# A hybrid decoder layer on eight cores: one tile at a time against list-scheduled groups of four tiles with transposes by DMA and streamed weights

## The reference

```python
def layer_norm(x, g, b):
    xf = x.astype(jnp.float32)
    mu = jnp.mean(xf, axis=-1, keepdims=True)
    var = jnp.mean(jnp.square(xf - mu), axis=-1, keepdims=True)
    y = (xf - mu) * lax.rsqrt(var + EPS) * g.astype(jnp.float32) + b.astype(jnp.float32)
...
def hgrn2_chunk(state, inp):
...
    b = jnp.cumsum(log_f, axis=2)                    # inclusive log decay within chunk, <= 0
...
    o_inter = jnp.einsum('bhck,bhkv->bhcv', q * jnp.exp(b), state)
...
    a_diag = jnp.einsum('bhntk,bhnsk,bhntsk->bhnts', qs, ks, decay)
    o_diag = jnp.einsum('bhnts,bhnsv->bhntv', a_diag, vs)
...
    a_off = jnp.einsum('bhntk,bhnsk->bhnts', q_off, k_off)
    o_off = jnp.einsum('bhnts,bhsv->bhntv', a_off, v)
    o = o_inter + (o_diag + o_off).reshape(B, H, C, V)
    new_state = state * jnp.exp(b_last)[..., None] + jnp.einsum(
        'bhck,bhcv->bhkv', k * jnp.exp(b_last[:, :, None] - b), v)
    return new_state, o
...
def hgrn2_mixer(q_raw, f_raw, i_raw, g_raw, lower_bound, norm_g, valid):
...
    q = jax.nn.silu(q_raw.astype(f32))
    fg = lower_bound + (1.0 - lower_bound) * jax.nn.sigmoid(f_raw.astype(f32))
    m = valid[None, :, None]
    log_f = jnp.where(m, jnp.log(fg), 0.0)           # pad slots: identity transition
...
    k = jnp.where(m, 1.0 - fg, 0.0)                  # input gate tied to forget gate; pads write nothing
...
    o = o * lax.rsqrt(jnp.mean(o * o, axis=-1, keepdims=True) + EPS) * norm_g.astype(f32)
    gate = jax.nn.silu(g_raw.astype(f32)).reshape(B, P, HG_HEADS, HG_V)
    return (o * gate).reshape(B, P, HG_VW).astype(q_raw.dtype)
...
def swa_sink_attention(q_raw, k_raw, v_raw, sinks, pos):
...
    q = rope(q_raw.reshape(B, P, ATT_HEADS, HEAD_DIM), pos).astype(f32)
    k = rope(k_raw.reshape(B, P, ATT_KV_HEADS, HEAD_DIM), pos).astype(f32)
    v = v_raw.reshape(B, P, ATT_KV_HEADS, HEAD_DIM).astype(f32)
    scale = HEAD_DIM ** -0.5
...
    band_ok = (key_pos >= N_META) & (key_pos <= qp) & (qp - key_pos < WINDOW)
    meta_ok = meta_pos <= qp                       # meta tokens always visible (causally)
...
    p = jax.nn.softmax(jnp.concatenate([s_meta, s_band, sink], axis=-1), axis=-1)
...
    o = (jnp.einsum('bnhgqm,bmhd->bnqhgd', p_meta, v_meta)
         + jnp.einsum('bnhgqk,bnkhd->bnqhgd', p_band, v_band))
    return o.reshape(B, P, ATT_QW).astype(q_raw.dtype)
...
        proj = h @ w_in[l]                                   # single combined input projection
        hq, hf, hi, hg, aq, ak, av, gates = jnp.split(proj, split_idx, axis=-1)
        y_hg = hgrn2_mixer(hq, hf, hi, hg, lbs[l], hg_norm_g[l], valid) @ w_branch_hg[l]
        y_att = swa_sink_attention(aq, ak, av, attn_sinks[l], pos) @ w_branch_attn[l]
        g_hg, g_att = jnp.split(jax.nn.sigmoid(gates), N_BRANCH, axis=-1)
        mix = (g_hg * y_hg + g_att * y_att) @ w_out[l]
        h = layer_norm(ALPHA * h + mix, ln1_g[l], ln1_b[l])
        a, u = jnp.split(h @ w_ffn_in[l], 2, axis=-1)
        h = layer_norm(ALPHA * h + (jax.nn.silu(a) * u) @ w_ffn_out[l], ln2_g[l], ln2_b[l])
    return h[:, BLOCK:]
```

## Time and profile before

| | |
|---|---|
| runs | 4988.68, 4994.0 and 4994.34 us, median 4994.0 |
| the profiled execution | 5015.8 us (slowest of eight cores; 4970.0 to 5015.8) |
| PE busy | 4311.7 us, 86% |
| DVE busy | 2566.4 us, 51% |
| ACT busy | 1584.3 us, 32% |
| POOL busy | 557.2 us, 11% |
| DMA | 243.09 MB, 48 GB/s on the mean |

### The profile page before, as it was taken

How to read it: one execution, slowest core, us unless ns; L and a number is a source line. 1 busy time by engine, 2 the same in 40 slices (tenths; PEclk the granted TensorE clock), 3 DMA queues, 4 the chain that set the end, 5 groups by cost and what they waited for, 6 DMA issues and landing times.

```text
span 5015.8 us, 65133 instructions; the slowest of 8 cores (4970.0 to 5015.8 us)
## 1 busy us (share of the span) xinstructions
PE 4311.7 (86%) x22787; PEld 2046.9 (41%) x22787; DVE 2566.4 (51%) x4615; ACT 1584.3 (32%) x2827; POOL 557.2 (11%) x677
## 2 busy tenths in 40 slices
PE   0798888888888888888888873999999999999998
PEld 0344444444444444444444431444444444444443
DVE  2355666666665666666665641444444444444444
ACT  2344444444444444444444430111111111111111
POOL 0011111111111111111111110000000000000000
PEclk9678999999999999999999986999999999999999
DMA  8006321000001000000000005111111111111110
GB/s 254 15 34 90 71 53 49 34 34 33 27 31 34 34 34 34 34 34 34 28 29 34 34 20 178 42 43 42 43 43 42 43 43 43 46 47 51 44 49 34
DMA packets 86113, 243.09 MB, mean 48 GB/s; under 512 B 10160, under 2 KB 19632, under 8 KB 84928
## 3 DMA queue, kind: packets, MB, share of 16 engines
q1 hardware_dynamic: 84448, 221.62, 13.1%
q0 software_dynamic: 1344, 17.30, 2.6%
HBM read 172.30 MB, written 101.19 MB: 55 GB/s over the span
## 4 chain that ended last, share of the span: by engine, by line
PE 69%; DVE 9%; ACT 8%; issue 8%; DMA 4%; POOL 1%; DVEq 0%; SPq 0%; ACTq 0%; POOLq 0%
PE ps L425 19%; PE ps L995 13%; PE ps L966 11%; PE ps L969 11%; PE ps L803 5%; PE ps L776 2%; PE ps L409 2%; ACT L503 2%; PE ps L506 1%; ACT hbf L476 1%; ACT mT L413 1%; ACT hT L413 1%; PE ps L509 1%; ACT thG L764 1%; PE ps L516 1%
## 5 line engine op out<-in xcount | busy, mean ns | idle before, releaser
L425 PE MATMUL ps<-win,hT 128*128 128x512 bf16 (+1 forms) x5160 | 1329.3, 409 | 55.9 <-ACT hT L413 55.9
L425 PEld LDWEIGHTS ps<-win,hT 128*128 128x128 bf16 x5160 | 516.7, 106 | 635.0 <-issue 280.9
L966 PE MATMUL ps<-hTg,wfi 128*128 128x512 bf16 x2816 | 666.9, 380 | 98.9 <-issue 78.3
L974 ACT ACTIVATE tha<-ps 128x512 bf16<-128x512 f32 x352 | 210.5, 598 | 1655.6 <-PE ps L969 1607.5
L995 PE MATMUL ps<-wfo,gT 128*128 128x512 bf16 x2816 | 631.1, 388 | 42.7 <-DVE gT L981 38.8
L969 PE MATMUL ps<-hTg,wfi 128*128 128x512 bf16 x2816 | 665.6, 379 | 0.0
L977 DVE SCALAR_TENSOR_TENSOR s2b<-tha,ps 128x512 f32<-128x512 bf16 x352 | 241.9, 687 | 669.3 <-ACT tha L974 669.2
L966 PEld LDWEIGHTS ps<-hTg,wfi 128*128 128x128 bf16 x2816 | 274.6, 98 | 435.8 <-issue 108.2
L995 PEld LDWEIGHTS ps<-wfo,gT 128*128 128x128 bf16 x2816 | 279.4, 100 | 394.4 <-issue 78.1
L969 PEld LDWEIGHTS ps<-hTg,wfi 128*128 128x128 bf16 x2816 | 275.7, 98 | 332.9 <-issue 1.1
L803 PE MATMUL ps<-wo,mT 128*128 128x512 bf16 x1024 | 240.9, 390 | 59.3 <-ACT mT L413 59.3
(11 more groups left out here) (174 smaller groups left out, 5539.6 us busy)
## 6 DMA issues: line engine op xcount, KB each, us to landing
h_scr<-r SPq DMA_DIRECT2D x64, 512.0 KB, 2.6
h1in<-h_scr SPq DMA_DIRECT2D x64, 512.0 KB, 4.1
x_1<-x SPq DMA_DIRECT2D x32, 512.0 KB, 3.7
x_0<-x SPq DMA_DIRECT2D x32, 512.0 KB, 3.8
h1T_scr<-h1T SPq DMA_DIRECT2D x64, 256.0 KB, 2.2
hTg<-h1T_scr SPq DMA_DIRECT2D x64, 256.0 KB, 2.7
y_out<-rr_0 SPq DMA_DIRECT2D x32, 512.0 KB, 2.9
y_out<-rr_1 SPq DMA_DIRECT2D x32, 512.0 KB, 2.9
```

Of the source, the lines that this page charges most:

```text
L425: inst = e.matmul(psb(bk)[:, 0:ncols], hTt[:, c, :], win_sb[:, c, col0:col0 + ncols], start=(c == 0), stop=(c == 7))
L966: inst = e.matmul(psb(ba)[:, 0:ntok], wfi_sb[:, c, j * 128:(j + 1) * 128], hTg[gi][:, 0:ntl, c, :], start=(c == 0), stop=(c == 7))
L974: S2.op("act", lambda e: e.activation(out=tha[ai][:, 0:ntok], in_=psb(ba)[:, 0:ntok], func=AF.Tanh, scale=0.5), reads=[Bbank2[ba]], writes ...
```

## The change

The kernel is written anew; reference, inputs and the split over cores stay.

**Order.** Every operation carries a cost in ns and its place in the program. `schedule` is a list scheduler: it keeps a clock per engine and takes, among the operations that are ready by then, the earliest in the program for which a PSUM bank is free (pools: pairs of banks for projections, a pair for the attention, single banks for the recurrence). Costs are constants in the code. The program's order from which it starts treats groups of four tiles, 16 of them: recurrence (`stage2`) and attention (`stage3`) of group g are merged with the first projections of group g+1 (`s12`), then come the gates and branches of g (`stage4`) with the first norm of g+2 (`stage0`), then the output projection (`stage5`). The meta tokens are handled apart, 16 rows alone.

**Layout.** Query and forget projections (`hgrn_qf`), gates and branches are computed channel-major, 128 channels by the 512 tokens of a group, so that the outputs `mT` and the inputs of the recurrence need no transposes. The cumulative decay is a `tensor_tensor_scan` on VectorE. The chunk of the recurrence is 128 tokens in one step. The attention's products with the values have 64 outputs by 512 columns; a matrix of ones gives the denominators in the same form, the sink is a row of `Em`, and the division is a reciprocal of 128 x 512 and a multiplication.

**Transposes.** What stays token-major is transposed by DMA, four a tile in pass 1 (`hT`, `qkT`, `ktok`, `ogT`) and one in pass 2 (`h1T`), all issued by SP.

**Weights.** DMAs on GpSimd's queue cast all weights to bf16 in HBM or SBUF. `wv`, `whg`, `waq`, `wakv` and `wo` stay in SBUF in pass 1, `wfo` in pass 2. Query, forget, gate, branch and FFN-in weights are read from HBM again for each group, through a ring of 11 slots (`ring`).

**Boundary.** The fence between the passes is gone. Pass 1 stores the residual sum, and the norm after it is now in pass 2 (`stage6`). ScalarE computes Silu in one step there, and VectorE one operation per block instead of two. The output product of the FFN is cut in two halves over j.

```diff
-            def transposes(src_fn, n, dst2, BdstT, Bsrc, evac_eng, bk):
...
-                def pe_fn(e):
-                    inst = None
-                    for i in range(n):
-                        inst = e.transpose(pv[:, i * 128:(i + 1) * 128], src_fn(i), ident[:])
-                    return inst
...
-                if evac_eng == "act":
-                    S.op("act", lambda e: e.copy(out=dst2, in_=pv[:, 0:n * 128]), reads=[Bbank[bk]], writes=[BdstT])
...
-                S.op("pe", lambda e: e.matmul(psb(bP), T64, lnf[:], start=True, stop=True),
-                     reads=[Blnf, B_const], writes=[Bbank[bP]])
...
-                S.cur = lB1 = []
-                if t < NT:
-                    do_B1(t)
-                S.cur = lA = []
-                if t + 1 < NT:
-                    do_A(t + 1)
-                extra = []
-                if t >= min(6, NT):
-                    take = len(cv_ops) if t == NT else 3
-                    extra, cv_ops[:] = cv_ops[:take], cv_ops[take:]
-                order += merge3([lB2, lB1, lA, extra]) if PIPELINE else (lB2 + lB1 + lA + extra)
...
+    def schedule(self, pools):
...
+                for s, i, o in heapq.nsmallest(12, cand[e]):
+                    t, _ = bank_at(o)
+                    if t is None:
+                        continue
+                    t = max(t, free[e])
+                    if o.tab is not None and cur not in o.tab:
+                        t = max(t, o.ready + self.PATIENCE)
+                    if pick is None or t < pick[0]:
+                        pick = (t, o)
+                    if t <= free[e]:
+                        break
...
+    def cast_dma(dst, src, writes, nbytes):
...
+        dma(lambda e: e.dma_start(out=dst, in_=src), [], list(writes) + [cvB[k]], "cv%d" % k, nbytes, cost=1100,
+            eng="pool")
...
+    def ring_load(nslots, src, Bsrc):
+        at = rg["at"]
+        if at + nslots > RING:
+            at = 0
+        rg["at"] = at + nslots
+        bs = Bring[at:at + nslots]
+        dma(lambda e: e.dma_start(out=ring[:, at:at + nslots, :].rearrange("p a b -> p (a b)"), in_=src), Bsrc, bs,
+            "rg%d" % at, nslots * 2048 * 128)
+        flat = ring[:, at:at + nslots, :].rearrange("p a b -> p (a b)")
...
+    def stage0T(t, g, s):
+        kb = t % 4
+        dst = hT[g % 2]
+        dma(lambda e: e.dma_start_transpose(out=dst[:, :, s * 128:(s + 1) * 128], in_=hbf[kb][:]), [Bhbf[kb]],
+            [BhT[g % 2][s]], "hT%d_%d" % (g % 2, s), 262144, cost=1200)
...
+        dma(lambda e: e.dma_start_transpose(out=qkT[kt][:], in_=qkr[kr][:]), [Bqkr[kr]], [BqkT[kt]], "qkT%d" % kt,
+            163840, cost=1200)
...
+    def hgrn_qf(h, g, w, Bw, ntok):
...
+        S.op("dve", lambda e: e.tensor_tensor_scan(out=lb_[:, 0:ntok], data0=rm[:, 0:ntok], data1=lb_[:, 0:ntok],
+                                                   initial=0.0, op0=ALU.mult, op1=ALU.add),
+             [Blb, Brm], [Blb], cost=2 * dve(512))
...
+    def stage2(t, g, s):
...
+        dma(lambda e: e.dma_start_transpose(out=ktok[i2][:], in_=kd[:, s, :, :].rearrange("p h t -> p (h t)")), Bkd,
+            [Bktok[i2]], "kt%d" % i2, 131072, cost=1200)
...
+        def fR(e):
+            inst = None
+            for h in range(4):
+                inst = e.tensor_scalar(out=R32[:, h, :], in0=Tst[:, h, :], scalar1=dap[:, h:h + 1],
+                                       scalar2=cie[:, h:h + 1], op0=ALU.mult, op1=ALU.mult)
...
+        dma(lambda e: e.dma_start_transpose(out=ogT[:, :, s * 128:(s + 1) * 128], in_=og[i2][:]), [Bog[i2]],
+            [BogT[s]], "ogT%d" % s, 131072, cost=1200)
...
+    def stage3(t, g, s):
...
+        def fpv(e):
+            inst = None
+            for i, (E, _, v, _, on, _) in enumerate(kinds):
+                for q in range(2):
+                    inst = e.matmul(bank(P)[q * 64:(q + 1) * 64, :], v[:, q * 64:(q + 1) * 64], E[:, q, :],
+                                    start=(i == 0), stop=(i == n - 1))
+                for q in range(2):
+                    inst = e.matmul(bank(P, 1)[q * 64:(q + 1) * 64, :], on[:], E[:, q, :], start=(i == 0),
+                                    stop=(i == n - 1))
+            return inst
...
+        S.op("dve", lambda e: e.reciprocal(out=rd[:], in_=bank(P, 1)), [P.sub[1]], [Brd], cost=3380)
+        S.op("dve", lambda e: e.tensor_tensor(out=aoT[:, :, s * 128:(s + 1) * 128],
+                                              in0=bank(P).rearrange("p (j q) -> p j q", j=4),
+                                              in1=rd[:].rearrange("p (j q) -> p j q", j=4), op=ALU.mult),
+             [P.sub[0], Brd], [BaoT[s]], cost=dve(512))
...
+    def stage4(c, g, nt):
+        w, Bw = ring_load(3, wgb_d[c], Bwgb[c])
...
+        def fg_(k):
+            def f(e):
+                inst = None
+                for kc in range(8):
+                    inst = e.matmul(bank(P, k)[:, 0:ntok], w[:, kc * 256 + k * 128:kc * 256 + (k + 1) * 128],
+                                    hTg[:, kc, 0:ntok], start=(kc == 0), stop=(kc == 7))
+                return inst
+            return f
...
+        def fy(e):
+            inst = None
+            for h in range(4):
+                inst = e.matmul(bank(Y)[:, 0:ntok], w[:, 2048 + h * 128:2048 + (h + 1) * 128], ogT[:, h, 0:ntok],
+                                start=(h == 0), stop=(h == 3))
+            for h in range(4):
+                inst = e.matmul(bank(Y, 1)[:, 0:ntok], w[:, 2560 + h * 128:2560 + (h + 1) * 128], aoT[:, h, 0:ntok],
+                                start=(h == 0), stop=(h == 3))
+            return inst
...
+        S.op("dve", lambda e: e.scalar_tensor_tensor(out=m12[:], in0=thG[i2][:], scalar=1.0, in1=pair(Y),
+                                                     op0=ALU.add, op1=ALU.mult), [BthG[i2]] + Y.sub, [Bm12],
+             cost=dve(1024))
+        S.op("pool", lambda e: e.tensor_tensor(out=mT[:, c, :], in0=m12[:, 0:512], in1=m12[:, 512:1024],
+                                               op=ALU.add), [Bm12], [BmT[c]], cost=1210)
...
+    def stage5(t, g, s):
...
+        S.op("dve", lambda e: e.scalar_tensor_tensor(out=xb[:], in0=pair(P), scalar=0.5 / ALPHA, in1=xb[:],
+                                                     op0=ALU.mult, op1=ALU.add), P.sub + [Bxb], [Bxb],
+             cost=dve(1024))
+        dma(lambda e: e.dma_start(out=r_d[t * 128:(t + 1) * 128, :], in_=xb[:]), [Bxb], [Br_d[t]], "rs%d" % k, 524288)
...
+    for g in range(NG):
+        la = recs([(stage2, t, g, s) for s, t in enumerate(groups[g])])
+        lb = recs([(stage3, t, g, s) for s, t in enumerate(groups[g])])
+        lc = s12(g + 1) if g + 1 < NG else []
+        ops += merge(la, lb, lc)
+        l4 = recs([(stage4, c, g, len(groups[g])) for c in range(8)])
+        l0 = recs([(stage0, t, g + 2, s) for s, t in enumerate(groups[g + 2])]) if g + 2 < NG else []
+        ncv = len(ffn_cv) if g == NG - 1 else (4 if g >= 1 else 0)
+        cv, ffn_cv[:] = ffn_cv[:ncv], ffn_cv[ncv:]
+        ops += merge(l4, l0, cv)
+        l5 = recs([(stage5, t, g, s) for s, t in enumerate(groups[g])])
+        l0 = recs([(stage0T, t, g + 2, s) for s, t in enumerate(groups[g + 2])]) if g + 2 < NG else []
+        ops += merge(l5, l0)
...
+    def stage6(t, g, s):
...
+        dma(lambda e: e.dma_start_transpose(out=h1T[g % 2][:, :, s * 128:(s + 1) * 128], in_=h1b[kb][:]), [Bh1b[kb]],
+            [Bh1T[g % 2][s]], "h1T%d_%d" % (g % 2, s), 262144, cost=1200)
...
+    def ffn_in(j, g, nt, gslots):
+        w, Bw = ring_load(2, wfi_d[j], [Bwfi_d[j]])
...
+        S.op("act", lambda e: e.activation(out=sl[i][:, 0:ntok], in_=bank(P)[:, 0:ntok], func=AF.Silu), [P.sub[0]],
+             [Bsl[i]], cost=act(512), tab="S")
...
+            for a in range(0, NJ, 11):
+                js = list(range(a, min(a + 11, NJ)))
+                S.op("pe", fo(n, js), [BgT[gslots[j]] for j in js] + [Bwfo[j] for j in js], [P.sub[n]],
+                     cost=MM(len(js)))
...
+    S.schedule({"P": [0, 2], "S": [4], "H": [6, 7], "F": [0, 2, 4, 6]})
```

1813 lines of the change are left out of this document (963 added, 850 removed).

## The result

The changed kernel takes 4247.45 us as a median of four runs against 4994.17 (4233.4 without the run at 4699.98); the ratio is 0.849, 95% interval 0.846 to 0.853.

The account below looks back on a forecast made before the run. TensorE was taken to bound both passes, with VectorE nearly equal outside pass 1's gates. Start 75, groups 2000, turn 15, pass 2 1864 and tail 12 sum to 3966 us, as a median 3950; range 3780 to 4090, with (a) to 4400.

Parts of the forecast that it names:

- The groups: Pass 1: 125 us a group, from 33 for gates and branches plus 78 at 85% busy TensorE (92); 16 groups 2000.
- VectorE: Pass 1: VectorE's work sums to 21.2 us a tile (18.5 to 23), 85 a group, below TensorE's 111.
- The start: Before the steady groups: weights load while TensorE has work for about half; 75 us over the steady pace (50 to 120).
- The turn: Between the passes: only the normalisation of four tiles stands in the way; 15 us (5 to 30) instead of 78.
- Pass 2 and tail: Pass 2 at 116.5 us a group (114.5 to 121), 1864 in all; tail after the last product 12 us.
- The signs: Listed measurements that would show the forecast right, such as groups of 120 to 130 us and TensorE near 88%.
- (a): Rival: VectorE and the chain bind pass 1; a group takes 130 to 150 us, total 4190; chance 0.30.
- (b): Rival: DMA transposes bind SP's queue; at 12 us each total 5270; chance 0.05 up to the old time, 0.07 beyond.
- (c): Rival: denser work lowers the clock on all cores, groups at 145 and 140 us, total 4640; chance 0.04.
- (d): Rival: weights stream slower, in pass 2 at 100 GB/s instead of 145, 168 us a group, total 4770; chance 0.03.

Follow-up runs that it names:

- e1: The changed kernel with each cast of the FFN weights made to wait for its group's first merge: 4202.6 us, ratio 0.841.
- e5: As e1, but the scheduler is told that the FFN casts move no bytes: 4226.1 us, ratio 0.847.
- e9: As e5, with two casts under way at a time instead of four: 4182.1 us, ratio 0.838.
- e12: As e11, with one cast under way at a time instead of two: ratio 0.837.
- e13: The changed kernel with FFN casts held for their group's first merge (priced), one cast at a time, and xB at the end of pass 1's memory: 4090.7 us, 0.818.
- e11: As e10, with the residual buffers xB laid at the end of pass 1's memory, no longer under h1: ratio 0.838.
- e10: As e9, with a group's four FFN casts waiting for its last merge instead of its first: 4218.1 us, ratio 0.845.

## Why the prediction was right or wrong

**The groups: right in mechanism, 5.8 us too low each.** The split was: gates 33, the rest 78 of TensorE's work at 85% busy. Measured: 37.3 and 93.5, with TensorE at 83% of the rest (the gates' stretch runs at full clock and is longer because it holds 177 products and not the 152 that I counted, so the sum of both is the better measure). TensorE's busy time is 115.0, forecast 111. The attention's products were 0.9 us a tile cheaper than I took (a pair at 0.22, below the lower bound of 0.31 that I read from the scores); so 107.4 would have been due, 7.6 less than measured. Most of the 7.6 is the clock, 0.94 outside the gates, which I had priced only as a rival. The attention's query projection shows it in one group, first behind a wait, then at once behind other products:

```profile
1240.40 0.59 PE L89 MATMUL ps<-waq,hT_88 128*128 128x512 bf16 x1 [5.64 <-ACT og_121 L933]
1240.78 3.19 PE L704 MATMUL ps<-waq,hT_88 128*128 128x512 bf16 x7
...
1274.36 1.67 PE L704 MATMUL ps<-waq,hT_88 128*128 128x512 bf16 x7
```

The same seven products take 3.19 us at the lower of the two levels (1.2 GHz) and 1.67 at the upper; added up over seven groups, what products took beyond their time at full clock is some 5 to 6 us a group, an estimate from the rows. The idle time, 15.8 us a group, is 1.8 over the 14 in the forecast (92 - 78). So the 5.8 us too many are -3.6 for the attention, +7.6 and +1.8; for the whole of pass 1 that is 93 us.

**VectorE: right in the sum, partly by luck.** It is busy 85.2 us a group, forecast 85. But the forecast added up durations of single operations (its terms as listed give 20.9 a tile, not 21.2), and measured so a tile takes 22.7 (635.7 us for 28 tiles); the busy time is less because operations overlap. The reciprocal (2.6 taken, 3.35 measured, inside 0.69 to 4.4) and the four products with two scalars (0.22 taken, 0.44 on the mean) were under; the scan (1.4 taken, 1.19 and 1.66) was right on the mean.

**The start: the step that failed.** I took 11 and 14 MB at the pace of one row, let TensorE work half of that time, and wrote that the streams fit, with landings that grow. Three things were wrong in it. The FFN's 17 MB stood nowhere in this term, because I read their place in the program and not in the order in which GpSimd issues them: some 86 us (e1). Transfers were priced by bytes, while with four casts in flight loads of x and the slowest transposes land late, and the first tiles go through x, a norm, a transpose and a product one after another: the first branch product comes 20 us earlier with half as many, 64 with a quarter, 27 of which the next group loses again (e5, e9, e12). And TensorE did not work half: 55.6 of the first 200 us. What remains of the 263 after these steps is not settled; in e13 start and casts together are still 203 us (2252.9 less 16 groups of 128.1).

**The turn: mis-sized.** 15 taken (5 to 30), 36.8 measured. The norms that I named were not the wait; the loads ahead of them stood behind `xB`, over which `h1` lies in memory (e11). That lies in the code, and no row of before could show it.

**Pass 2 and tail: right, a little over.** 114.2 us a group against 116.5, just under the range of 114.5 to 121; TensorE was busy for 500 of 500 us, so the gaps that I had left in (116.5 - 113.9) were not there.

**The signs.** TensorE at 88% (804.74 of 915.63), VectorE's 21 us a tile and the reciprocal came as I wrote. Groups of 120 to 130 us, a clock of 0.96 or more, pass 2 at 115 to 118 a group and less than 30 us between the passes did not.

**The rivals.** (a) gave 4190, and its range held the result, but it did not happen: VectorE was at 81% outside the gates, and taking the reciprocal away (10.7 us) gave 3.5. The number agreed by way of the start, and that is luck. (b) fell: a transpose holds SP for 1.17 to 1.35 us, 16 of them 19 to 22 of a group's 131, where a plain load holds it for 0.38; `hT` (256 KB) lands in 3.2 to 4.3 us, plain transfers of 512 KB in 3.6 to 7.5. The Trainium skill's rule (Advanced Engine Details and Errata, X-Bar Transpose (TRN2)) that they are as fast as regular transfers agrees roughly with the landing, and not with the queue, where one costs three plain ones. (c) fell in pass 2, at a clock of 1.00 with all eight cores busy. The Trainium skill's rule that I cited (TensorE: Matmul & The Clock Gate, Part 1) doesn't show in this execution either. (d) held off in both passes; it came back in small where large casts ran beside the ring (e5).

## What to carry to other kernels

Where a scheduler starts what is ready, read the order on each queue, DMA issues of background work above all: what has no operand is started first. A mean DMA share of 0.57 (e5) did not tell how late a transfer came that an engine needed at once: price background DMAs by the waits of what lands behind them, keep few in flight, and look for the in-order engine that stands at a late load while others wait behind it. Between two passes, look at which buffers lie over which.

## What the runs showed of the hardware

- A cast that writes 512 KB cost a group 3.5 us beside the gates and 3.6 behind them, at a DMA share of 0.57 and 0.59 (e5, e10). One of half the size cost nothing beside the gates (130.8 us a group in e5) and 1.2 behind them (135.7 in e10).
- In the changed kernel's first 100 us casts took the DMA engines for 56.5 us for 7.60 MB written; all other transfers together 35.3 for 9.14.
- Two products with 64 outputs, to the two halves of the same bank, run side by side: 0.22 us for both, as long as one full product.
- The reciprocal costs (3351 - 193)/504 = 6.3 ns a column beyond its fixed part, with 193 ns for 8 columns; I had estimated 4.75.
